# Index differences of four tokens from one product, filler products in picks and scatters, and an earlier first load of index rows

## The reference

```python
idx = jnp.take_along_axis(cand_idx..., pos, axis=-1)   # 8 heads x 16 experts a token
gate = jax.nn.softmax(best, axis=-1)
def blk(args):
    xb, ib, gb = args
    u = U[ib]
    hid = jax.nn.gelu(jnp.einsum('td,thkd->thk', xb, u))
    v = Vt[ib]
    return jnp.einsum('thk,thkd->td', gb * hid, v)
```

## Time and profile before

| what | us |
|---|---|
| median of 3 runs | 2200.37 |
| lowest and highest | 2198.88, 2211.62 |
| profiled execution, its own time | 2205.52 |
| span of the profile | 2203.8 |
| mean granted TensorE clock | 0.886 of full speed |

### The profile page before, as it was taken

One profiled execution on the slowest core, in us unless ns is written; L12 is line 12 of the kernel. 1 busy time (PEld: TensorE's weight loads), 2 busy tenths in 40 slices (PEclk: granted clock), 3 DMA queues, 4 the chain that ended last, 5 costly groups with the idle time before them and its releaser, 6 DMA issues.

```text
span 2203.8 us, 28931 instructions
## 1 busy us (share of the span) xinstructions
PE 2114.2 (96%) x10823; PEld 1849.9 (84%) x10823; DVE 1496.6 (68%) x1970; ACT 818.3 (37%) x956; POOL 826.3 (37%) x626
## 2 busy tenths in 40 slices
PE   7999999999999999999999799998899999999997
PEld 6988998787888899887887688888789888888886
DVE  5465764557555576889876455556522899999998
ACT  4345333443434442222221232335433444444444
POOL 1010410000000001666554555566500667888873
PEclk9999999999999999999999755555555999999999
DMA  6555444445555555999999766677601799999996
GB/s 211 180 184 172 153 141 156 153 138 187 190 189 193 184 199 191 389 409 409 399 362 363 281 219 209 205 240 254 225 2 58 282 390 384 388 404 406 386 393 244
DMA packets 172772, 557.65 MB, mean 253 GB/s; under 512 B 17360, under 2 KB 18400, under 8 KB 171616
## 3 DMA queue, kind: packets, MB, share of 16 engines
q1 hardware_dynamic: 114160, 287.94, 37.3%
q0 software_dynamic: 58480, 267.94, 32.6%
HBM read 551.10 MB, written 4.72 MB: 252 GB/s over the span
## 4 chain that ended last, share of the span: by engine, by line
PE 81%; DMA 8%; DVE 5%; issue 3%; ACT 2%; POOL 1%; DVEq 0%; SPq 0%; POOLq 0%; ACTq 0%
PE acc L1895 7%; PE acc L1897 6%; PE acc L1896 6%; PE scr L2192 6%; PE acc L2157 5%; PE scr L2157 5%; PE scr L2221 4%; PE acc L1878 4%; PE acc L1881 4%; PE acc L1880 4%; PE acc L2275 3%; PE scr L2276 3%; PE acc L2276 3%; PE scr L2275 3%; PE scr L2277 3%
## 5 line engine op out<-in xcount | busy, mean ns | idle before, releaser
L1094 DVE TENSOR_TENSOR w_lo<-raw,w_hi 128x2048 fp32r<-128x2048 f32 x136 | 314.7, 2314 | 279.2 <-ACT w_hi L741 278.1
L741 ACT ACTIVATE w_hi<-raw 128x2048 fp32r<-128x2048 f32 x136 | 260.1, 1914 | 404.8 <-PE acc L1897 273.3
L697 POOL DMA_INDIRECT starts<-in_v_gather,expert x256 | 355.7, 1389 | 127.4 <-DVE X L1800 80.7
L674 POOL DMA_INDIRECT slots<-in_u_gather,expert x256 | 244.9, 957 | 337.8 <-ACT slots L951 94.3
L1613 DVE SCALAR_TENSOR_TENSOR slots<-slots,acc 128x1280 f32<-128x1280 f32 x192 | 282.4, 1484 | 87.0 <-DMA slots<-in_u_gather,expert 85.3
L1032 ACT ACTIVATE v_hi<-v_raw 128x1344 fp32r<-128x1344 f32 x128 | 170.5, 1332 | 259.8 <-PE scr L2277 205.6
L1800 DVE SCALAR_TENSOR_TENSOR X<-starts,weight,X 128x704 f32<-128x704 f32 x256 | 242.0, 945 | 0.3
L1895 PE MATMUL acc<-w_hi,hT_hi 128*128 128x512 f32 x576 | 227.3, 395 | 2.5 <-DVE w_lo L1094 2.5
L1897 PE MATMUL acc<-w_hi,hT_lo 128*128 128x512 f32 x576 | 225.1, 391 | 0.0
L1896 PE MATMUL acc<-w_lo,hT_hi 128*128 128x512 f32 x576 | 224.8, 390 | 0.0
L1817 DVE TENSOR_TENSOR v_lo<-v_raw,v_hi 128x1344 fp32r<-128x1344 f32 x128 | 199.3, 1557 | 9.4 <-issue 7.4
(11 more groups left out here) (321 smaller groups left out, 4225.5 us busy)
## 6 DMA issues: line engine op xcount, KB each, us to landing
raw<-in_w_in SPq DMA_DIRECT2D x88, 1024.0 KB, 5.0
v_raw<-in_v_dense SPq DMA_DIRECT2D x128, 672.0 KB, 7.5
ub<-in_u_dense SPq DMA_DIRECT2D x128, 384.0 KB, 7.0
raw<-in_w_o SPq DMA_DIRECT2D x16, 1024.0 KB, 5.1
raw<-in_peer_wq SPq DMA_DIRECT2D x16, 1024.0 KB, 5.4
raw<-in_w_a_up SPq DMA_DIRECT2D x8, 1024.0 KB, 5.2
raw<-in_w_b_up SPq DMA_DIRECT2D x8, 1024.0 KB, 5.2
slots<-in_u_gather,expert POOLq DMA_INDIRECT x256, 6.8
```

The source lines that it names most:

```text
L674: pool.indirect_dma_start(slots[j][:, :], None, u_gather[:, :], bass.IndirectOffsetOnAxis(ap=expert[:, t, k:k + 1], axis=0)).then_inc(row_ ...
L697: pool.indirect_dma_start(starts[j][:, :], None, v_gather[:, :], bass.IndirectOffsetOnAxis(ap=expert[:, s // NSEL, s % NSEL:s % NSEL + 1], ...
L741: a.activation(w_hi[:, m % 2, :, :], raw[:, m % 2, :, :], ACT.Copy).then_inc(hi_ready, 1)
L1094: v.tensor_tensor(w_lo[:, m % 2, :, :], raw[:, m % 2, :, :], w_hi[:, m % 2, :, :].bitcast(fp32), ALU.subtract).then_inc(lo_ready, 1)
```

## The change

One piece of index rows is now loaded in another order, the four numbers of each token one below the other: 16 rows for four tokens, with the row of ones 17. Against it stand wide test tables of 17 rows and 512 columns (`table_i`, `table_j`), which VectorE builds in groups 28 to 30 (`marks`, `table`). So one product of 512 columns gives the differences of four tokens, where four of 128 columns did. `squares_j` needs the old order, so in the picks (`h < CHUNKS // 2`) each piece is loaded in both. `warm` puts filler products on TensorE, whose result is overwritten: one of 256 columns in each pick, three of 512 in each of the first 32 scatters, one of 256 in each of the last. The memset of ones is done in two parts (`ones(True)` behind group 31, without a wait for the dense U products, and `ones(False)` as before), and the first piece is loaded after the first. The iota for the tables is made by GpSimd later.

```diff
+RA_AT, RB_AT = (31, 31.5, 199), (13, 120, 197)
+CHUNKS = 2 * NT * P // (4 * SC)
+R_ROWS = 1 + 4 * SC
+WARM_PICK, WARM_FIRST, WARM_LAST = 2 * P, 4 * P, 2 * P
...
                 for r in range(4):
+                    s = slice(s0 + SC * r, s0 + SC * r + SC)
+                    sp.dma_start(rows_a[h % RPIECES][32 * r + 1:32 * r + R_ROWS, :],
+                                 r_keep[t, s, :, :].rearrange("s c k -> (s c) k")).then_inc(r_landed[h % RPIECES], 16)
+                    if h < CHUNKS // 2:
+                        sp.dma_start(rows_b[h % RPIECES][32 * r + 1:32 * r + 5, :].rearrange("c (s k) -> c s k", s=SC),
+                                     r_keep[t, s, :, :].rearrange("s c k -> c s k")).then_inc(r_landed[h % RPIECES], 16)
...
-            sp.wait_ge(ones_ready, 1)
-            sp.sem_inc(granted_w, 1)
-            for h in range(4 * 8):
+            for h in range(CHUNKS):
+                if h < 2:
+                    sp.wait_ge(ones_ready, h + 1)
+                    sp.sem_inc(granted_w, 1)
                 load_rows(h)
...
                 if q == FOUR:
                     pool.wait_ge(unit_done, UNIT0[G_END])
+                    g.iota(iota_p[:, :], [[1, P]], base=0, channel_multiplier=0, allow_small_or_imprecise_dtypes=True
+                           ).then_inc(consts_ready, 1)
...
+            def table(c, j):
+
+                r = 1 + 4 * c + 2 * j
+                to = (table_j if j else table_i)[:, c * P:(c + 1) * P]
+                link(v.tensor_scalar(part, centred, tests[:, r:r + 1], -2.0, ALU.mult, ALU.mult))
                 link(v.scalar_tensor_tensor(out=total, in0=curve, scalar=tests[:, 0:1], in1=part,
                                             op0=ALU.mult, op1=ALU.add))
+                link(v.tensor_scalar(to, total, tests[:, r + 1:r + 2], 1.0 if j else FAR, ALU.add, ALU.mult))
...
-            def ones():
+            def ones(first):
 
                 dve.wait_ge(cen_stored, 16 * NT)
-                dve.wait_ge(u_used, BLOCKS)
-                for n in range(RPIECES):
-                    last = v.memset(rows[n][:, :], 1.0)
+                if not first:
+                    dve.wait_ge(u_used, BLOCKS)
+                for room in (rows_a[0], rows_a[1], rows_b[0]) if first else (rows_a[2], rows_b[1], rows_b[2]):
+                    last = v.memset(room[:, :], 1.0)
                 last.then_inc(ones_ready, 1)
...
+                if i == CEN_GROUP[1]:
+                    marks()
+                if i in (CEN_GROUP[1] + 1, CEN_GROUP[1] + 2):
+                    for c in range(SC):
+                        table(c, i - CEN_GROUP[1] - 1)
+                if i == CEN_GROUP[1] + 3:
+                    ones(True)
...
+            def warm(to, n):
+
+                if n:
+                    t_.matmul(to[:, 0:n], table_i[:, 0:P], table_i[:, 0:n], start=True, stop=True)
...
-                for c in range(SC):
-                    t_.matmul(to[:, c * P:(c + 1) * P], room[g5, c * P:(c + 1) * P], tests_i[g5, :], start=c == 0, stop=False,
-                              skip_group_check=True)
+                warm(to, WARM_PICK)
+                t_.matmul(to, room, test, start=True, stop=False, skip_group_check=True)
...
-                for c in range(SC):
-                    last = t_.matmul(square_a[:, c * P:(c + 1) * P], room[g5, c * P:(c + 1) * P], tests_i[g5, :],
-                                     start=True, stop=True)
-                last.then_inc(a_squared, 1)
+                if w < BATCHES:
+                    warm(square_a, WARM_FIRST)
+                t_.matmul(square_a, room, test_a, start=True, stop=True).then_inc(a_squared, 1)
                 if w:
                     pe.wait_ge(b_hot_ready, w)
-                for c in range(SC):
-                    last = t_.matmul(square_b[:, c * P:(c + 1) * P], room[g5, c * P:(c + 1) * P], tests_j[g5, :],
-                                     start=True, stop=True)
-                last.then_inc(b_squared, 1)
+                if w < BATCHES:
+                    warm(square_b, WARM_FIRST)
+                    warm(square_b, WARM_FIRST)
+                else:
+                    warm(square_b, WARM_LAST)
+                t_.matmul(square_b, room, test_b, start=True, stop=True).then_inc(b_squared, 1)
```

More of the change, by code:

```diff
@@ L267, in build @@
     x_keep = nc.dram_tensor("x_keep", (P, NT, D), fp32, kind="Internal").ap()
-    r_keep = nc.dram_tensor("r_keep", (NT, 4, P, P), fp32, kind="Internal").ap()
+    r_keep = nc.dram_tensor("r_keep", (NT, P, 4, P), fp32, kind="Internal").ap()
     ctx = ExitStack()
@@ L280, in build @@
         fox_mask = sb("fox_mask", [P, S])
+        vecT = sb("vecT", [P, 16])
+        table_at = (nc.sbuf_base + 31) // 32 * 32
         vec = sb("vec", [16, P])
-        vecT = sb("vecT", [P, 16])
         wff = sb("wff", [P, KD, H])
@@ L286, in build @@
         c_tok = sb("c_tok", [P, NT, H])
-        lb = sb("lb", [P, 4, H])
         stat = sb("stat", [P, 6, 16])
@@ L295, in build @@
         arena_at = (nc.sbuf_base + 31) // 32 * 32
-        sb("arena", [P, 202 * KB])
+        sb("arena", [P, 203 * KB + 64])
         def at(name, kib, shape, dt=fp32):
@@ L311, in build @@
         cen = at("cen", 198, [4, P])
-        rows = [at(f"rows{n}", kib, [SC * P]) for n, kib in enumerate(R_AT)]
+        rows_a = [at(f"rows_a{n}", kib, [P]) for n, kib in enumerate(RA_AT)]
+        rows_b = [at(f"rows_b{n}", kib, [SC * P]) for n, kib in enumerate(RB_AT)]
+        table_i = nc.alloc_sbuf_tensor_at("table_i", [P, SC * P], f32r, offset=table_at)
+        table_j = at("table_j", 201.25, [SC * P], f32r)
+        lb = at("lb", 201.5, [4, H])
         hidT = at("hidT", 15, [NT, P])
@@ L352, in build @@
         weight, gate = carve("weight", NT, NSEL), carve("gate", NSEL)
-        gateT = carve("gateT", NT, P)
+        gateT, iota_p = carve("gateT", NT, P), carve("iota_p", P)
         hot_a, hot_b = at("hot_a", 101, [2, SC, P]), at("hot_b", 105, [2, SC, P])
@@ L364, in build @@
         topv, topf, topi = spare("topv", 16, TOPK), spare("topf", 16, TOPK), spare("topi", 16, TOPK, dt=u32)
-        expert = at("expert", 200.5, [NT, NSEL], u32)
+        expert = at("expert", 200.25, [NT, NSEL], u32)
         bpos, bposf, rest = spare("bpos", 3, NSEL, dt=u32), spare("bposf", 3, NSEL), spare("rest", 2 * P)
-        tests_i, tests_j = wff_hi[:, :, :].rearrange("p k h -> p (k h)"), wff_lo[:, :, :].rearrange("p k h -> p (k h)")
-        centred = wff[:, :, :].rearrange("p k h -> p (k h)")
+        tests = stat[:, 0:2, :].rearrange("p a b -> p (a b)")
         q_hg, k_hg = Z1[:, 0:8 * S], Z1[:, 8 * S:16 * S]
@@ L395, in build @@
         neg_c = ff_room[0:H, 0:S]
-        iota_p = ff_room[:, S + P:S + 2 * P]
         acc = ctx.enter_context(nc.psum_tensor("acc", [P, 2, 2 * GW], fp32))
@@ L537, in keep_rows @@
                 sp.sem_inc(granted_w, 1)
-                sp.dma_start(r_keep[t].rearrange("c s k -> s c k"), cen[:, :, :]).then_inc(cen_stored, 16)
+                sp.dma_start(r_keep[t].rearrange("s c k -> s c k"), cen[:, :, :]).then_inc(cen_stored, 16)
             def load_rows(h):
@@ L1651, in _, with marks @@
             link(v.tensor_copy(iota16_ps, iota16[:, :]))
[L1653 to L1661, removed]
+            centred, part, total = hot[:, 0:P], hot[:, P:2 * P], hot[:, 2 * P:3 * P]
+            def marks():
+                dve.wait_ge(consts_ready, 3)
+                link(v.tensor_reduce(tests, ident[:, :].rearrange("p (g r) -> p r g", r=32), AX.X, ALU.add))
+                link(v.tensor_scalar(centred, iota_p[:, :], float(P // 2), None, ALU.subtract))
+                link(v.tensor_tensor(curve, centred, centred, ALU.mult))
+            def table(c, j):
+                r = 1 + 4 * c + 2 * j
+                to = (table_j if j else table_i)[:, c * P:(c + 1) * P]
+                link(v.tensor_scalar(part, centred, tests[:, r:r + 1], -2.0, ALU.mult, ALU.mult))
                 link(v.scalar_tensor_tensor(out=total, in0=curve, scalar=tests[:, 0:1], in1=part,
                                             op0=ALU.mult, op1=ALU.add))
-                link(v.tensor_scalar(to, total, tests[:, c + 1:c + 2], FAR if n == 0 else 1.0, ALU.add, ALU.mult))
+                link(v.tensor_scalar(to, total, tests[:, r + 1:r + 2], 1.0 if j else FAR, ALU.add, ALU.mult))
             def centre(t):
@@ L1760, in _ @@
                     centre(CEN_GROUP.index(i))
+                if i == CEN_GROUP[1]:
[5 more added lines that the diff above has]
+                    ones(True)
                 if i == SELECT_FROM - 1:
-                    ones()
+                    ones(False)
                 if i in GATE_AT:
@@ L2173, in row_group @@
                 h = b // 4
-                pe.wait_ge(r_landed[h % RPIECES], 64 * (h // RPIECES + 1))
-                return rows[h % RPIECES][:, :].bitcast(f32r), slice(32 * (b % 4), 32 * (b % 4) + 5)
+                mine = range(h % RPIECES, h + 1, RPIECES)
```

(13 more changed lines are left out.)

7 lines of the change are left out of this document (1 added, 6 removed).

## The result

The change makes the kernel slower: 2256.27 us, the median of 4 runs (2246.04 to 2277.61), against 2205.99 for the kernel before on the same chip. The ratio is 1.0241, with a 95% interval of 1.0156 to 1.0326. The prediction said 2080 us, with a range of 2040 to 2178, and faster at 0.84. It was wrong in sign and outside its range. The profiled execution took 2256.53 us, its span is 2254.5, its mean granted clock 0.887.

A forecast was written before the change was run, and what follows sets the result against it. TensorE's products at half clock were taken to bound picks and scatters, with gathers next. Terms of 51 + 12 + 5 + 51 + 9 - 4 = 124 us off 2205.5 gave 2082, forecast as 2080, range 2040 to 2178.

The forecast's parts named there:

- One product for four differences: In scatters, eight differences fall from 1.89 to 0.86-1.08 us at 1.2 GHz, 1.03 to 0.46-0.58 at 2.4; picks win nothing at 1.2.
- Fillers in TensorE's own time: In picks and scatters, fillers lose TensorE time (0.21 us a pick at 1.2 GHz) and pay only through the clock.
- Picks at 2.4 GHz: In the picks, the full clock mostly holds and 16 groups take 152 us for 203: 51 won.
- First scatters: In the first 32 scatters, at 2.4 GHz GpSimd's pace rules and 14 groups take 119 us for 131: 12 won.
- the tail: Between first and last scatters, where the second token tile's hidden values are finished: 5 us won at 2.4 GHz.
- Last scatters: In the last 32 scatters, residual products lift the clock; 1.95 us a batch, 67 us for 118: 51 won.
- First index rows: Ahead of the picks, loading the first index rows earlier cuts a 13 us gap to about 4: 9 won.
- What is late next: Ahead of the picks, once rows come early, the last eviction and first activation set the start, leaving about 4 us.
- Tables: In groups 29 and 30, VectorE's eight test tables take 8.4 us, partly covered by the wait for gathers: 4 lost.
- (a): Rival: clock lost in picks and first scatters, back with residual products; 2110-2145 us in part (0.20), 2145-2186 in full (0.13).
- (c): Rival: fillers' exposed weight loads at 1.2 GHz slow picks and first scatters; 26 us slower, 2226 us; chance 0.04.
- (b): Rival: fillers do nothing for the clock anywhere; from 38 us won to 15 lost, middle 2190; chance 0.10.

The follow-up runs named there:

- e1: The changed kernel with all filler products left out and the 17-row products kept; 2124.98 us, ratio 0.9624 to the kernel before.
- e11: The changed kernel with fillers in the picks alone, 256 columns between squares and differences as in the change; 2202.42 us, ratio 0.9979 to before.
- e6: The changed kernel with 44 dense products ahead of the picks and a 256-column filler ahead of each pick's squares, none in the scatters; 2139.57 us.
- e5: The changed kernel without fillers, plus 44 products of 512 columns in the wait ahead of the picks; 2126.08 us, ratio 0.9623 to before.
- e12: As e5, but the picks' whole-array products read unstrided columns (wrong activations, so hidden values differ); 2122.96 us, ratio 0.9613 to before.
- e8: The changed kernel without fillers, the first two chunks of index rows fetched late as in the kernel before; 2127.01 us, ratio 0.963 to before.
- e7: The changed kernel without fillers, ScalarE computing the first two one-hots one group earlier, ahead of the sum; 2124.97 us, ratio 0.9618 to before.

## Why the prediction was wrong

*One product for four differences.* The mechanism was right. In the last scatters both differences cost 0.67 us at 1.00 in e1, above the 0.46 to 0.58 forecast and below the 1.03 of before, and no filler is needed to hold the clock. In the picks I forecast nothing at 1.2 GHz and 0.32 us a pick was won: squares and differences run side by side in both kernels, and the pair went from 1.04 us to 0.73.

*Fillers in TensorE's own time: the first step that failed.* I added "up to 0.11 per product where a load may be exposed" at 1.2 GHz. Measured at 0.50 is 0.72 for a product of few rows and 512 columns that stands between whole-array ones, 0.29 over the 0.43 of the earlier trace rows, and 0.51 for the filler, 0.30 over its 0.21. So a pick took 3.99 us, not 3.10 to 3.43, a first scatter 5.02, not 4.16 to 4.71 (1550.06 to 1555.08). The earlier trace rows was the wrong row to size it by: dense products with the whole array on both sides hide their loads. The rows of the weight loads show the difference, in the kernel after:

```profile
1342.94 0.29 PEld L2206 LDWEIGHTS scr<-table_i 128*128 128x128 f32 x1 [0.44 <-issue]
1343.45 0.28 PEld L2220 LDWEIGHTS scr<-table_i,rows_a 17*128 17x128 f32 x1 [0.22 <-issue]
```

and in the dense products of the kernel before:

```profile
443.17 0.33 PEld L1895 LDWEIGHTS acc<-w_hi,hT_hi 128*128 128x128 f32 x1
```

In the pick the loads of the filler and of the differences start at 1342.94 and 1343.45, together with their own products, and their 0.29 and 0.28 us match the surcharge. In the dense stage the load of L1895 starts at 443.17, 0.43 us ahead of its product at 443.60.

I also summed a pick's products one after the other, without seeing that two of them ran together in the kernel before. The sum for the changed pick doesn't suffer by that, as the filler does part them, but it hid what this place costs: of the filler's 1.24 us, 0.98 come from its place (e11 against e6). By the starts some 0.7 of this is the second product of few rows, which runs beside the first where they are neighbours, and the rest the filler's own load.

The Trainium skill has the rule on the page "TensorEngine Tiling (Array Packing)", under "Key Properties": tiles of the array work independently, their weight loads too, and a change of the tiling mode drains the engine. The traces agree: starts 0.01 us apart in e1, 0.72 us each with a whole-array product between. That a drain is the mechanism, the runs don't show.

*Picks at 2.4 GHz, 51 won: the second step that failed, twice.* The clock didn't come, nor would it have paid. It was lost even with a start at 1.00, and with the filler (e5, e6). The price was mis-sized: 1.09 for eight whole-array products was taken from the scatters, but a pick's read a strided operand and take 1.93 at 1.00 against 2.03 at 0.50 (e5); unstrided they take the 1.09 of the scatters (e12). A pick gains 0.39 us from the full clock, not 1.4. By an estimate from 2.36 at 1.00 without filler and 3.07 before, 64 picks at the full clock would have won 45 us at most, so the 51 were never there. The rule of the Trainium skill's page "TensorE: Matmul & The Clock Gate" that I set beside it was no better guide, read by the busy row: in e5 the clock fell in the second pick, with TensorE busy in every microsecond around the fall.

*First scatters.* Forecast 12 won and 5 in the tail, measured 22 lost with the tail: 5.02 us a batch at 0.50, by the same loads as in the picks. Without fillers the stage takes 141 us for 148 although a batch takes only 3.2: there VectorE's weights for a batch are what TensorE waits for (29.8 us of waits in e1), and VectorE itself waits 26.0 us there for gathered rows to land.

*Last scatters.* The lift by the residual products came as forecast. The size was off on both sides: 2.25 us a batch with the filler instead of 1.95, and the clock lost again; 1.74 to 1.76 without. Without the filler the stage wins 51 us. That this equals the forecast, which was made for batches with the filler, is chance.

*First index rows, 9 won:* 2 at most (e8). "What is late next" named the first activation, but not what stands ahead of it in ScalarE's queue, and behind that comes the next group's (e7). *Tables, 4 lost:* nothing visible; the last U column's product ends between 1228 and 1234 us in the thirteen profiles with the tables, and at 1233 before.

Of the rivals, (a) had the clock right up to the last scatters: 0.50 in picks and first scatters, back only with the residual products. (c), at 0.04, named what that costs, and its test, a pick of over 3.4 us. It was sized 30 us too small, since it took 0.11 for each exposed load where 0.28 to 0.30 were measured; over a pick's three products that is 0.56 us, 36 us in 64 picks. The range left (c) out, and (c)'s own 2226 would not have reached the result. Two slips in the recorded sums change none of this: the upper end of (b) adds up to 33 won, not 38, and 124 off the median of 2200 would be 2076, not 2080.

Open stays why the clock falls again in the last scatters in all profiles with a filler and in none of the changed kernel without one, and why picks with strided columns lose it while those with unstrided ones held it until a wait. The runs show only that it is so.

## What to carry to other kernels

Before adding a product to a sequence on TensorE, look at the starts of its neighbours: two that use few rows of different partition groups may be running as one, and a whole-array product between them makes three steps of one. Size what a higher clock is worth from the operation itself, with its own operand layout, not from one of the same shape elsewhere. And take off an addition that is meant to change a state and run the rest alone: here the change without its fillers is 4% faster than before (e1), and with them about 2% slower.

## What was not expected of the hardware

A pick's eight whole-array instructions read 128 columns each, one element in every 512 bytes. From start to start they take 0.22 us at 1.00 and 0.22 at 0.50 (e5, first and second pick), so the full clock gives them nothing; what it gives a pick lies mainly in the two products of few rows, 0.43 us (e5) for 0.73 (e1). With neighbouring elements the same instructions take 0.11 us at 1.00 (e12) and 0.21 in the scatters at 0.50 (after).

A filler of 256 columns in the last scatters cost about 0.5 us a batch at 1.00, twice the 0.23 of a dense product of 512 columns. By the starts of after (from 1710.29) 0.32 of this is the filler's own step; the rest is that the two differences around it take 0.42 us each, where they took 0.34 and 0.33 as neighbours in e1.
